# Norms over features through token columns: eight-column roots and reciprocals, spread back by TensorE

## Chip, cores and metric

The kernel runs on one core of a Trainium2 chip. The metric is the device time of one execution in microseconds (us), the median of several runs.

## The reference

Two transformer blocks follow each other on 1024 tokens of 1024 features, with 256 context tokens beside them. The norms and the residual sums around them are, cut down:

```python
def rms_norm(x, g):
    y = x * rsqrt(mean(x * x, axis=-1) + 1e-6)
    return y * g

# first block, its end
x = x + g1 * (y @ w_out)
x = x + g2 * swiglu(modulate(rms_norm(x, norm_ffn_g), sh2, sc2), w_ffn_in, w_ffn_out)
x = rms_norm(x, final_g)
# second block
h  = modulate(rms_norm(x, norm1), shift1, scale1)
hc = modulate(rms_norm(ctx, norm1), cshift, cscale)
# attention, state-space and grid branches of h and hc, then
x = x + gate1 * merged_branches
h2 = modulate(rms_norm(x, norm2), shift2, scale2)
x = x + gate2 * conv_ffn(h2, ...)
out = rms_norm(x, final_norm)
```

Each norm takes a mean over the features of one token, and there is a root and a reciprocal for each token.

## The kernel before

Features lie on the 128 partitions in eight blocks `k`, tokens along the free dimension, so x is 128 x 8192 and is worked on in pieces of 512 tokens (`LAT` is the two halves `n0` = 0 and 512; `ALL` adds the 256 context tokens in front). A sum over features is thus a sum over partitions and blocks. Each engine runs a program written by hand, stage after stage (`sp`, `act`, `dve`, `pool`, `pe` at the end of the file); the engines meet only at semaphores, `wait_ge(*stage.engine.after(key))`. An engine takes its instructions strictly in that order.

`SumSq` is the norm's sum. ScalarE squares block k of x into one of three buffers (`sqr`, a ring: a buffer is taken again when its last reader is through); GpSimd adds it to the square of block k-1 and so frees that one; when the eighth is added, TensorE multiplies the sum with a matrix of ones, so that the sum over partitions stands in every partition of a bank, 128 x 512; VectorE makes mean plus epsilon in `rsx`, ScalarE the root, VectorE the reciprocal, all on 512 columns.

The stages around it are: `op1` (output product, adds to x), `ffn1` (first feed-forward), `fn` (final norm of the first block, norm of the context and of the second block), `sx` (first products of the second block), and at the end `op2`, `ffn2` and the last norm (`last_dve`). In both products the float weights are cut into two parts, high by ScalarE (`wfh<-wslot`), low by VectorE (`wfl<-wslot,wfh`), into a ring of two, and each product is three matmuls. `Ffn` walks over tiles: `("u", f, 0)` and `("u", f, 1)` upward, then eight `("d", f, m)` downward for each group of four f; the last group has only two, so that its tiles are short: 12 matmuls. In these last eight tiles x is final block by block, and `SumSq` runs beside them. On ScalarE a tile m first cuts the weights of tile m+1, then squares block m of x:

```python
if i + 1 < len(self.tiles):
    self.cut_act(e, self.tiles[i + 1])
for n0, n in LAT:
    if kind == "d":
        if f + FP >= NF:
            self.ss.act(e, m, n0, n)
```

At a feed-forward's start `norm_dve` makes, for each half, the reciprocal, then for each k a product `t` (from `rsx`), which ScalarE shifts and rounds to `h`, and the rest `l`; TensorE's first tile waits for `l` of each k.

In `fn` VectorE first norms x in place with final_g (`x<-x,par,rsx`); the normed x is written to memory (`xspill`, read again by `op2`); the context is loaded, squared, summed; the normed x is squared and summed again; then the products `h<-x,gs,rsx` and ScalarE's shifts `h<-h,mod`. The first products of `sx` (`dtT`: 32 rows for context, half 0, half 1) follow on TensorE.

## Time and profile before

| | us |
|---|---|
| runs | 5033.08, 5028.90, 5030.50 |
| median | 5030.5 |
| profiled execution | 5029.09 |
| its span (core 0) | 5026.8 |
| TensorE busy in it | 4401.3 (88%) |
| VectorE busy | 2383.7 (47%) |
| ScalarE busy | 1396.0 (28%) |
| GpSimd busy | 983.2 (20%) |
| granted TensorE clock, mean | 0.935 of full |

The profiled execution is one run with the hardware profiler on; its span runs from the first to the last instruction, and the time adds what lies around it. Busy shares are over the whole span, so what an edit is worth must be read where it stands.

### The profile page before, as it was taken

Reading aid. Unit: us, or ns where it says so; the run is one execution under the profiler, and the core shown is the slowest. Engines: PE = TensorE matmul, PEld = TensorE weight load, DVE = VectorE, ACT = ScalarE, POOL = GpSimd, SP = SyncE. Lnnn points to the kernel's source line nnn. Section 1 sums busy time; section 2 is a strip of 40 time slices with the busy share of each in tenths; the row PEclk is TensorE's granted clock in tenths of the full one; section 3 lists DMA queues with packets and bytes.
Section 4 is the critical chain, followed back from the end, with each engine's and each line's share of the span. In section 5 each row is a group of like instructions: output and inputs, shape, how many; then the busy total and the mean of one; then the engine's idle time right before and its main releaser. Section 6 shows DMA issues by size and latency. Waiting matters only on the chain. (4 is left out here: it accounts for less than half of the span.)

```text
span 5026.8 us, 45510 instructions
## 1 busy us (share of the span) xinstructions
PE 4401.3 (88%) x18317; PEld 3044.0 (61%) x18317; DVE 2383.7 (47%) x3755; ACT 1396.0 (28%) x2601; POOL 983.2 (20%) x769
## 2 busy tenths in 40 slices
PE   7984788988899999587979998888797988999997
PEld 3454773675688888345554455555464656888885
DVE  2767745334555553335261105472675634333334
ACT  3431222112211111233231104352453533222222
POOL 0003443330244431305160100001000011000001
PEclk9996899999999999787979999999898999999998
DMA  5010032212233332102021110102000022111111
GB/s 180 25 59 17 28 103 90 59 59 73 66 109 113 114 105 61 58 27 75 17 76 34 34 43 18 37 22 80 13 20 23 20 70 71 51 49 44 51 42 59
DMA packets 245746, 288.34 MB, mean 57 GB/s; under 512 B 18112, under 2 KB 208896, under 8 KB 244256
## 3 DMA queue, kind: packets, MB, share of 16 engines
q1 hardware_dynamic: 227536, 203.51, 13.2%
q0 software_dynamic: 14880, 76.68, 4.8%
q10 hardware_dynamic: 3120, 5.24, 0.3%
...
## 5 line engine op out<-in xcount | busy, mean ns | idle before, releaser
L193 PE MATMUL bank<-h,wslot 128*128 128x512 f32 (+3 forms) x2096 | 906.1, 573 | 58.0 <-DMA wslot<-in_w_in 29.3
L193 PEld LDWEIGHTS bank<-h,wslot 128*128 128x128 f32 (+1 forms) x2096 | 382.2, 192 | 382.6 <-issue 364.9
L193 PE MATMUL bank<-hT,wslot 128*128 128x512 f32 (+3 forms) x1136 | 462.6, 564 | 38.0 <-DMA hT<-hspill 20.4
L193 PEld LDWEIGHTS bank<-hT,wslot 128*128 128x128 f32 (+1 forms) x1136 | 212.6, 190 | 266.3 <-issue 237.6
L193 PE MATMUL bank<-ffn1h,wfh 128*128 128x512 f32 x704 | 280.4, 398 | 18.8 <-DVE ffn1l L211 17.8
L193 PE MATMUL bank<-ffn2h,wgh 128*128 128x512 f32 x704 | 276.8, 393 | 17.3 <-DVE ffn2l L211 16.7
L211 DVE SCALAR_TENSOR_TENSOR x<-bank,mod,x 128x512 f32<-128x512 f32 x224 | 163.4, 745 | 246.8 <-PE bank L193 246.6
L193 PE MATMUL bank<-ffn1l,wfh 128*128 128x512 f32 x704 | 275.8, 392 | 0.0
L193 PE MATMUL bank<-ffn1h,wfl 128*128 128x512 f32 x704 | 275.2, 391 | 0.0
L193 PE MATMUL bank<-ffn2l,wgh 128*128 128x512 f32 x704 | 275.1, 391 | 0.0
L193 PE MATMUL bank<-ffn2h,wgl 128*128 128x512 f32 x704 | 275.1, 391 | 0.0
L205 DVE TENSOR_TENSOR wfl<-wslot,wfh 128x1024 fp32r<-128x1024 f32 (+2 forms) x92 | 155.4, 1689 | 159.8 <-ACT wfh L202 159.8
L205 POOL TENSOR_TENSOR sq<-sq 128x512 f32<-128x512 f32 (+1 forms) x91 | 112.2, 1233 | 427.2 <-ACT sq L202 423.2
L205 POOL TENSOR_TENSOR ffn2al<-ffn2ga,ffn2ah 128x512 fp32r<-128x512 f32 x44 | 57.4, 1305 | 662.0 <-ACT ffn2ah L202 662.0
L193 PEld LDWEIGHTS bank<-ffn1h,wfh 128*128 128x128 f32 x704 | 132.8, 189 | 52.3 <-DVE ffn1l L211 12.9
L226 DVE TENSOR_REDUCE at2a<-ffn1t 128x128 f32<-128x1024 f32 x72 | 143.2, 1988 | 44.2 <-POOL ffn1t L205 44.2
L193 PEld LDWEIGHTS bank<-ffn2h,wgh 128*128 128x128 f32 x704 | 132.7, 189 | 51.4 <-DVE ffn2l L211 13.0
L211 DVE SCALAR_TENSOR_TENSOR ffn2ga<-ffn2gw,par,ffn2ga 128x1024 f32<-128x1024 f32 x44 | 56.5, 1285 | 199.5 <-ACT ffn2ga L202 198.7
L193 PEld LDWEIGHTS bank<-ffn1h,wfl 128*128 128x128 f32 x704 | 133.0, 189 | 28.2
L193 PEld LDWEIGHTS bank<-ffn2h,wgl 128*128 128x128 f32 x704 | 132.9, 189 | 27.9
L193 PE MATMUL bank<-ffn1ah,wfh 128*128 128x512 f32 x352 | 142.8, 406 | 7.8 <-DVE wfl L205 7.1
L193 PEld LDWEIGHTS bank<-ffn2l,wgh 128*128 128x128 f32 x704 | 133.0, 189 | 26.7
...
## 6 DMA issues: line engine op xcount, KB each, us to landing
...
```

The lines of the kernel that those rows point to most:

```text
L193: return Counted() if counting[0] else self.q.matmul(o, l, r, start=start, stop=stop)
L205: return Counted() if counting[0] else self.q.tensor_tensor(o, a, b, op)
L211: return Counted() if counting[0] else self.q.scalar_tensor_tensor(o, a, s, b, op0, op1)
L226: return Counted() if counting[0] else self.q.reduce_sum(o, a, AX.X)
```

## The change

The sums change their form. TensorE now takes the squares as weights, 128 tokens at a time, and multiplies them with one column of ones: the result is a column of 128 token sums, one token per partition, and the 1024 tokens are eight columns of one bank. Mean, root and reciprocal work on 128 x 8. `spread_row` brings a column back to a row in every partition: the column, repeated 128 times, is the weight, the unit matrix the moving operand; four such matmuls fill 512 columns of a bank. The products then read this bank in place of `rsx`.

In `ffn1` (`SumSq2`) GpSimd's additions are left out: TensorE adds the blocks' columns up in one open bank during the last tiles, with two moving columns, ones and final_g squared, so that both the sum for the first norm and that for the norm after it come from the same squares. `fn` makes both reciprocals from them and applies both norms in one product; x stays as it was, is spilled in four parts during the last tiles, and `op2` norms it after loading it again. In both feed-forwards the squares of block m-1 are taken in tile m. In the products of `sx` the context comes last, and TensorE waits for each piece by itself. The context is loaded into buffers of `ffn1`, ahead of where the load stood.

```diff
+    def spread_row(e, rc, n0, n, b):
+        for c in range(n // 128):
+            i = e.matmul(b[:, hs[c]], rc[:, n0 // 128 + c:n0 // 128 + c + 1].to_broadcast([128, 128]), ident)
+        return i
...
+        def pe(self, e):
             for n0, n in LAT:
-                e.wait_ge(*self.st.pe.after("sum", n0))
-                e.tensor_scalar(rsx[:, n0:n0 + n], self.bk[n0 // 512][:, 0:n], 1.0 / D, EPS, OP.mult, OP.add).then_inc(self.st.dve("ms", n0), 1)
+                e.wait_ge(*self.st.pool.after("sq", n0, 7))
+                for c in range(4):
+                    i = e.matmul(bank[6][:, n0 // 128 + c:n0 // 128 + c + 1], sqr[self, n0, 7][:, hs[c]], ones[:, 0:1])
+                i.then_inc(self.st.pe("sum", n0), 1)
+                sqr.give((self, n0, 7), self.st.pe.now())
+            e.wait_ge(*self.st.dve.after("rs"))
+            for n0, n in LAT:
+                spread_row(e, self.rc, n0, n, self.row(n0)).then_inc(self.st.pe("row", n0), 1)
+        def dve(self, e):
+            e.wait_ge(*self.st.pe.after("sum", 512))
+            e.tensor_scalar(self.rc[:, :], bank[6][:, 0:8], 1.0 / D, EPS, OP.mult, OP.add).then_inc(self.st.dve("ms"), 1)
+            e.wait_ge(*self.st.act.after("rt"))
+            e.reciprocal(self.rc[:, :], self.rc[:, :]).then_inc(self.st.dve("rs"), 1)
...
+            e.wait_ge(*self.st.dve.after("ms"))
+            e.activation(self.rc[:, :], self.rc[:, :], AF.Sqrt).then_inc(self.st.act("rt"), 1)
+        def row(self, n0):
+            return bank[7 - n0 // 512]
 
         def rs(self, n0):
-            return self.inv.after("rs", n0)
+            return self.st.pe.after("row", n0)
...
+    class SumSq2(SumSq):
+        def pe_tile(self, e, k, n0, n):
+            if k == 0 and n0 == 0:
+                e.wait_ge(*fn.dve.after("g2"))
+                e.matmul(bank[6][:, 0:16], ident, C("offF", 112, 128), start=True, stop=False).then_inc(self.st.pe("zero"), 1)
+            e.wait_ge(*self.st.act.after("sq", n0, k))
+            for c in range(4):
+                at = (n0 // 128 + c) * 2
+                i = e.matmul(bank[6][:, at:at + 2], sqr[self, n0, k][:, hs[c]], gf2[:, k * 2:k * 2 + 2], start=False, stop=k == 7 and at == 14)
+            i.then_inc(self.st.pe("sum", n0, k), 1)
+            sqr.give((self, n0, k), self.st.pe.now())
...
+                prep(e, j)
...
-                self.ss_in.dve_inv(e, n0, n)
                 e.wait_ge(*d.after("gs"))
                 e.wait_ge(*self.ss_in.rs(n0))
                 for k in range(8):
                     tmp = self.tr.take(k, n0)
                     for ev in self.tr.freed(k, n0):
                         e.wait_ge(*ev)
-                    e.stt(tmp[:, 0:n], self.x(k, n0, n), gs1[:, k:k + 1], rsx[:, n0:n0 + n], OP.mult, OP.mult).then_inc(d("t", k, n0), 1)
+                    e.stt(tmp[:, 0:n], self.x(k, n0, n), gs1[:, k:k + 1], self.ss_in.row(n0)[:, 0:n], OP.mult, OP.mult).then_inc(d("t", k, n0), 1)
...
+                if kind == "d" and f + FP >= NF and m >= 2 and not self.conv:
+                    for n0, n in LAT:
+                        self.ss.pe_tile(e, m - 2, n0, n)
+            if self.conv:
+                self.ss.pe(e)
+            for m in () if self.conv else (6, 7):
+                for n0, n in LAT:
+                    self.ss.pe_tile(e, m, n0, n)
...
-                        if f + FP >= NF:
-                            self.ss.act(e, m, n0, n)
+                        if f + FP >= NF and m:
+                            self.ss.act(e, m - 1, n0, n)
...
-            self.ss.act_root(e)
+            for n0, n in LAT:
+                self.ss.act(e, 7, n0, n)
+            if self.conv:
+                self.ss.act_root(e)
...
+                    elif m % 2:
+                        e.wait_ge(*st.dve.after("x", f, m, 512))
+                        e.dma_start(io["xspill"][:, (m - 1) * NL:(m + 1) * NL], x1[:, (m - 1) * NL:(m + 1) * NL]).then_inc(xs_out(m), 16)
...
     def fn_sp(e):
+        barrier(e, at2.st)
+        for i in range(2):
+            e.dma_start(cx[i][:, :].rearrange("p (k t) -> p k t", t=CT), io["ctx2T"][:, i * 4:i * 4 + 4, :]).then_inc(cx_in(i), 16)
...
+        S = bank[6][:, 0:16].rearrange("p (c w) -> p c w", w=2)
+        e.tensor_scalar(rn1[:, :], S[:, :, 0], 1.0 / D, EPS, OP.mult, OP.add).then_inc(d("v1"), 1)
+        e.stt(gsc[:, :], ad2.mv[:, 8:16, 1], 1.0, P("norm1_2"), OP.add, OP.mult).then_inc(d("gsc"), 1)
+        e.stt(ggs[:, :], ad2.mv[:, 8:16, 0], 1.0, P("norm1_2"), OP.add, OP.mult).then_inc(d("gs"), 1)
+        e.wait_ge(*a.after("s1"))
+        e.reciprocal(rn1[:, :], rn1[:, :]).then_inc(d("r1"), 1)
+        e.wait_ge(*d.now())
+        e.tensor_tensor(rn2[:, :], S[:, :, 1], rn1[:, :], OP.mult).then_inc(d("q1"), 1)
+        e.wait_ge(*d.now())
+        e.tensor_tensor(rn2[:, :], rn2[:, :], rn1[:, :], OP.mult).then_inc(d("q2"), 1)
+        e.wait_ge(*d.now())
+        e.tensor_scalar(rn2[:, :], rn2[:, :], 1.0 / D, EPS, OP.mult, OP.add).then_inc(d("v2"), 1)
+        e.tensor_tensor(ggs[:, :], ggs[:, :], P("final_g"), OP.mult).then_inc(d("ggs"), 1)
+        e.wait_ge(*a.after("s2"))
+        e.reciprocal(rn2[:, :], rn2[:, :]).then_inc(d("r2"), 1)
+        e.wait_ge(*d.now())
+        e.tensor_tensor(rn12[:, :], rn2[:, :], rn1[:, :], OP.mult).then_inc(d("r12"), 1)
...
+        def ctx():
+            e.wait_ge(*fn.pe.after("cs"))
+            e.tensor_scalar(rcc, bank[4][:, 0:2], 1.0 / D, EPS, OP.mult, OP.add).then_inc(d("vc"), 1)
+            e.wait_ge(*a.after("sc"))
+            e.reciprocal(rcc, rcc).then_inc(d("rc"), 1)
         for n0, n in LAT:
-            e.wait_ge(*fn.dve.after("x", 7, n0))
-        e.dma_start(io["xspill"], x1[:, :]).then_inc(xs_out("out"), 16)
-        rms_c.pool(e)
-        for n0, n in LAT:
+            e.wait_ge(*fn.pe.after("row", n0))
             for k in range(8):
-                ss_f.pool(e, k, n0, n)
-    def fn_dve(e):
-        barrier(e, ffn1.st, ffn1.ss.st, at2.st)
-        for n0, n in LAT:
-            ffn1.ss.dve_inv(e, n0, n)
-            e.wait_ge(*ffn1.ss.rs(n0))
+                e.stt(hv2(k, CT + n0, n), X1(k, n0, n), ggs[:, k:k + 1], bank[7 - n0 // 512][:, 0:n], OP.mult, OP.mult).then_inc(d("h", CT + n0, k), 1)
+            if n0 == 0:
+                ctx()
+        e.wait_ge(*fn.pe.after("rowc"))
+        for k in range(8):
+            e.stt(hv2(k, 0, CT), XC(k), gsc[:, k:k + 1], bank[5][:, 0:CT], OP.mult, OP.mult).then_inc(d("h", 0, k), 1)
...
+    def fn_act(e):
+        d, a = fn.dve, fn.act
+        barrier(e, ffn1.st, at2.st)
+        e.wait_ge(*d.after("v1"))
+        e.activation(rn1[:, :], rn1[:, :], AF.Sqrt).then_inc(a("s1"), 1)
+        e.wait_ge(*cx_in.after(1))
+        def squares(ks):
+            for k in ks:
+                sq = sqr.take("cx", k)
+                for ev in sqr.freed("cx", k):
+                    e.wait_ge(*ev)
+                e.activation(sq[:, 0:CT], XC(k), AF.Square).then_inc(a("cq", k), 1)
+        squares(range(2))
+        e.wait_ge(*d.after("v2"))
+        e.activation(rn2[:, :], rn2[:, :], AF.Sqrt).then_inc(a("s2"), 1)
+        squares(range(2, 8))
+        e.wait_ge(*d.after("vc"))
+        e.activation(rcc, rcc, AF.Sqrt).then_inc(a("sc"), 1)
+        for n0, n in ALL[1:] + ALL[:1]:
             for k in range(8):
-                a = X1(k, n0, n)
-                e.stt(a, a, P("final_g", k, k + 1), rsx[:, n0:n0 + n], OP.mult, OP.mult).then_inc(fn.dve("x", k, n0), 1)
-        rms_c.dve(e)
-        e.wait_ge(*fn.dve.now())
-        ss_f.dve_mean(e)
-        for n0, n in LAT:
-            ss_f.dve_inv(e, n0, n)
-        nm_l.dve(e)
-        nm_c.dve(e)
-    def fn_act(e):
-        barrier(e, ffn1.st, ffn1.ss.st, at2.st)
-        e.wait_ge(*cx_in.after("in"))
-        rms_c.squares(e)
-        rms_c.roots(e)
-        for n0, n in LAT:
-            for k in range(8):
-                ss_f.act(e, k, n0, n)
-        ss_f.act_root(e)
-        nm_l.act(e)
-        nm_c.act(e)
+                e.wait_ge(*d.after("h", n0, k))
+                h = hv2(k, n0, n)
+                e.activation(h, h, AF.Identity, bias=ad2.mv[:, k, 0 if n0 else 1:1 if n0 else 2]).then_inc(a("h", n0, k), 1)
...
+        e.matmul(bank[4][:, 0:2], ident, C("offF", 112, 114), start=True, stop=False).then_inc(fn.pe("zero"), 1)
+        for k in range(8):
+            if k == 2:
+                e.wait_ge(*fn.dve.after("r12"))
+                for n0, n in LAT:
+                    spread_row(e, rn12, n0, n, bank[7 - n0 // 512]).then_inc(fn.pe("row", n0), 1)
+            e.wait_ge(*fn.act.after("cq", k))
+            for c in range(2):
+                i = e.matmul(bank[4][:, c:c + 1], sqr["cx", k][:, hs[c]], ones[:, 0:1], start=False, stop=k == 7 and c == 1)
+            i.then_inc(fn.pe(*(("cs", k) if k < 7 else ("cs",))), 1)
+            sqr.give(("cx", k), fn.pe.now())
+        e.wait_ge(*fn.dve.after("rc"))
+        spread_row(e, rcc, 0, CT, bank[5]).then_inc(fn.pe("rowc"), 1)
...
-                for n0, n in ALL:
+                for n0, n in ALL[1:] + ALL[:1]:
                     b = bk.take("dtT", n0)
+                    e.wait_ge(*h2_ready(n0))
...
+        def norm(e, j):
+            for n0, n in LAT:
+                a = X2r(j, n0, n)
+                e.wait_ge(*ln.pe.after("row", n0))
+                e.stt(a, a, P("final_g", j, j + 1), bank[7 - n0 // 512][:, 0:n], OP.mult, OP.mult).then_inc(ln.dve("x1", j, n0), 1)
+            e.wait_ge(*ln.dve.now())
+        op2.dve(e, lambda: x2_in.after("in"), norm)
...
+            spread_row(e, rn1, n0, n, bank[7 - n0 // 512]).then_inc(ln.pe("row", n0), 1)
...
-            ffn2.ss.dve_inv(e, n0, n)
             e.wait_ge(*ffn2.ss.rs(n0))
             for k in range(8):
                 a = X2r(k, n0, n)
-                e.stt(a, a, P("final_norm_2", k, k + 1), rsx[:, n0:n0 + n], OP.mult, OP.mult).then_inc(ln.dve("x", k, n0), 1)
+                e.stt(a, a, P("final_norm_2", k, k + 1), ffn2.ss.row(n0)[:, 0:n], OP.mult, OP.mult).then_inc(ln.dve("x", k, n0), 1)
```

How this moves instructions is seen in the order of each engine. TensorE, the end of `ffn1` (tile 2 and the beginning of tile 3; `wfh` and `wfl` are the cut weights), of the changed kernel:

```order
L193 MATMUL bank<-ffn1ah,wfh 128x512
L193 MATMUL bank<-ffn1al,wfh 128x512
L193 MATMUL bank<-ffn1ah,wfl 128x512
L193 MATMUL bank<-cst 128x16
L193 MATMUL bank<-gf,sq 128x2 x8
L193 MATMUL bank<-ffn1ah,wfh 128x512
L193 MATMUL bank<-ffn1al,wfh 128x512
L193 MATMUL bank<-ffn1ah,wfl 128x512
```

Between the matmuls of two tiles there now stand eight with two columns, for the squares of the block two tiles back; before, matmuls of 512 columns alone stood here.

ScalarE from the last cut of `ffn1` to the first shift (`rsx`, `rcx`, `rcs`, `gs` in this place are means of which the root is taken; `cx` is the context, which lies in `ffn1t` after the change), before:

```order
L202 ACTIVATE wfh<-wslot 128x256
L202 ACTIVATE sq<-x 128x512 x4
L202 ACT_TABLE_LOAD
L202 ACTIVATE rsx<-rsx 128x512 x2
L202 ACTIVATE sq<-cx 128x256 x8
L202 ACTIVATE rcx<-rcx 128x256
L202 ACTIVATE sq<-x 128x512 x16
L202 ACTIVATE rsx<-rsx 128x512 x2
L202 ACTIVATE h<-h,mod 128x512 x16
```

and of the changed kernel:

```order
L202 ACTIVATE wfh<-wslot 128x256
L202 ACTIVATE sq<-x 128x512 x6
L202 ACT_TABLE_LOAD
L202 ACTIVATE rcs<-rcs 128x8
L202 ACTIVATE sq<-ffn1t 128x256 x2
L202 ACTIVATE rcs<-rcs 128x8
L202 ACTIVATE sq<-ffn1t 128x256 x6
L202 ACTIVATE gs<-gs 128x2
L202 ACTIVATE h<-h,mod 128x512 x16
```

The sixteen second squares of x are gone, and the root for the context (`gs<-gs`) stands in front of the shifts. VectorE in front of `ffn1`, the piece of difference:

```order
-L208 TENSOR_SCALAR rsx<-bank 128x512 x2
+L208 TENSOR_SCALAR rcs<-bank 128x8
+L217 RECIPROCAL rcs<-rcs 128x8
+L214 COPY gf<-cst 128x8
+L205 TENSOR_TENSOR gf<-par 128x8
 L205 TENSOR_TENSOR wfl<-wslot,wfh 128x1024
 L211 SCALAR_TENSOR_TENSOR gs<-mod,par 128x8
-L217 RECIPROCAL rsx<-rsx 128x512
-L211 SCALAR_TENSOR_TENSOR ffn1t<-x,gs,rsx 128x512 x2
+L211 SCALAR_TENSOR_TENSOR ffn1t<-x,gs,bank 128x512 x2
```

The reciprocal moved from behind the weights' cut to ahead of it, and has 8 columns.

## Rows read from the trace of the kernel before

**Rows 1.** Windows view, all engines, over four stretches (us from the start).

```profile
core 0 of [0], span 5026.8 us
core 0: us, PE busy (x) PEld busy (x) DVE busy (x) ACT busy (x) POOL busy (x), PEclk, DMA share, GB/s
...
2047.40:2067.40 20.00, 15.30 (x49) 10.98 (x48) 10.45 (x12) 6.11 (x13) 10.21 (x8) 0.83 0.05 14
2074.00:2154.80 80.80, 8.71 (x11) 2.33 (x11) 43.61 (x53) 31.95 (x56) 25.95 (x25) 0.52 0.21 80
...
4998.70:5026.80 28.10, 3.70 (x4) 1.00 (x4) 19.43 (x21) 4.09 (x6) 3.78 (x3) 0.62 0.40 149
```

**Rows 2.** Timeline between the blocks, 2109 to 2155 us.

```profile
2109.74 9.70 POOL L205 TENSOR_TENSOR sq<-sq 128x512 f32<-128x512 f32 x7 [3.37 <-ACT sq L202]
...
2140.07 10.69 DVE L211 SCALAR_TENSOR_TENSOR h<-x,gs,rsx 128x512 f32<-128x512 f32 x16
2140.85 13.85 ACT L202 ACTIVATE h<-h,mod 128x512 f32<-128x512 f32 x24 [6.72 <-DVE h L211]
...
2154.80 29.87 PE L193 MATMUL bank<-h,wslot 128*32 128x256 f32 x80 [22.06 <-ACT h L202]
```

**Rows 3.** Timeline, one tile of ffn1's end, 2059 to 2064 us.

```profile
2059.29 0.50 PE L193 MATMUL bank<-ffn1ah,wfh 128*128 128x512 f32 x1 [2.00 <-DVE wfl L205]
...
2059.99 0.63 ACT L202 ACTIVATE sq<-x 128x512 f32<-128x512 f32 x1 [2.07 <-DVE x L211]
...
2060.70 1.28 POOL L205 TENSOR_TENSOR sq<-sq 128x512 f32<-128x512 f32 x1 [1.75 <-ACT sq L202]
...
2062.01 0.63 ACT L202 ACTIVATE sq<-x 128x512 f32<-128x512 f32 x1 [1.39 <-POOL sq L205]
...
2062.55 0.40 ACT L202 ACTIVATE wfh<-wslot 128x256 fp32r<-128x256 f32 x1
...
2062.98 1.31 DVE L205 TENSOR_TENSOR wfl<-wslot,wfh 128x256 fp32r<-128x256 f32 x1 [2.42 <-ACT wfh L202]
```

**Rows 4.** Timeline of TensorE at two places; the tile view of rt, its reciprocal.

```profile
371.00 1.06 PE L193 MATMUL bank<-cst,gg 128*128 128x128 f32 x8
...
1343.35 0.39 PE L193 MATMUL bank<-ffn1h,wfl 128*128 128x512 f32 x1
1343.58 0.28 PE L193 MATMUL bank<-cst,at2a 128*128 128x1 f32 x2
...
1344.03 0.40 PE L193 MATMUL bank<-ffn1l,wfh 128*128 128x512 f32 x1
...
L217 DVE RECIPROCAL rt<-rt x1: 203/203/203, 817.9 to 817.9; 128x8 f32<-128x8 f32 x1
```

**Rows 5.** Timeline in front of ffn1, 1295 to 1306 us.

```profile
1295.50 1.13 PE L193 MATMUL bank<-sq,cst 128*128 128x512 f32 x2 [2.04 <-POOL sq L205]
...
1297.39 0.63 ACT L202 ACTIVATE rsx<-rsx 128x512 f32<-128x512 f32 x1 [1.34 <-DVE rsx L208]
...
1300.87 1.23 DVE L205 TENSOR_TENSOR wfl<-wslot,wfh 128x1024 fp32r<-128x1024 f32 x1 [3.52 <-ACT wfh L202]
...
1302.09 3.34 DVE L217 RECIPROCAL rsx<-rsx 128x512 f32<-128x512 f32 x1
1305.54 1.41 DVE L211 SCALAR_TENSOR_TENSOR ffn1t<-x,gs,rsx 128x512 f32<-128x512 f32 x2
```

**Rows 6.** Timeline of the last 25 us.

```profile
5003.01 1.28 ACT L202 ACT_TABLE_LOAD   x1
5003.07 1.26 POOL L205 TENSOR_TENSOR sq<-sq 128x512 f32<-128x512 f32 x1 [0.74 <-ACT sq L202]
...
5018.80 5.39 DVE L211 SCALAR_TENSOR_TENSOR x<-x,par,rsx 128x512 f32<-128x512 f32 x8
```

**Rows 7.** VectorE's groups by line: products from the bank, and from SBUF.

```profile
L211 DVE SCALAR_TENSOR_TENSOR x<-bank,mod,x 128x512 f32<-128x512 f32 x224 | 163.4, 745 | 246.8 <-PE bank L193 246.6
...
L211 DVE SCALAR_TENSOR_TENSOR x<-x,par,rsx 128x512 f32<-128x512 f32 x32 | 21.6, 747 | 0.1
```

94 lines of the change are left out of this document (40 added, 54 removed).

## The prediction

> **What bounds the kernel now.** I read the windows view first. TensorE works for most of the span, so time can only leave where it stands still or runs slowly. Four such stretches touch the change [rows 1]: the last tiles of each feed-forward (49 matmuls in 20.0 us, about 12 to a tile, so 5.0 us a tile at granted clock 0.83), the 80.8 us between the blocks, in which TensorE is busy for 8.7 us, and the last 28.1 us. The same kind of gap, shorter, stands in front of each feed-forward [rows 5].
>
> The timeline then says what each gap waits for. Between the blocks the work is one line of dependences: a norm applied to x in place, a second set of squares, whose GpSimd sums of the first half alone take 9.70 us, reciprocals over 512 columns, then sixteen products (10.69 us) and ScalarE's shifts [rows 2]. TensorE restarts at 2154.80, after all 24 shifts. In the last feed-forward tiles a cycle runs over three engines [rows 3]: ScalarE squares (2059.99), GpSimd adds (to 2061.98), only then is a square buffer free for the next square (2062.01), behind which ScalarE cuts the next weights (2062.55), VectorE's cut ends at 2064.29, and TensorE, which finished the tile before, starts. A half costs 2.02 us of square and sum. In front of a feed-forward a reciprocal of 3.34 us stands between the weight cut and the first product, and another between the halves [rows 5].
>
> **A, op1 into ffn1.** The order rows show two 512-column reciprocals replaced by one of 8 columns. A reciprocal on 8 columns took 0.203 us [rows 4]. The sum becomes four matmuls per half. The one-column matmuls of the trace are the same thing: two records of 128x1 push the matmul after next to 0.68 us behind, where two spacings of 0.23 are 0.45, so a matmul costs 0.23 and four cost 0.9 [rows 4]; the old sum took 1.13. The mean takes about 0.2 instead of 0.7 us, the root about 0.25 instead of 0.63. The last root then ends near 1296.9 instead of 1298.02. Behind it on ScalarE stand a table load, two small activations and the cut; all move 1.1 us up. VectorE's cut still follows, but the first product follows it directly: the 3.45 us from 1302.09 to 1305.54 go [rows 5]. The second half starts with no reciprocal: 3.4 us more, in full, since VectorE's products pace TensorE in both halves. The spread of the reciprocal (eight matmuls, two records each, of the form that shows 8 records in 1.06 us [rows 4]: some 2 us) lies beside the cut; without that cover it would cost 1.0 for the first half. A = 1.1 + 3.45 + 3.4 = **7.9 us**.
>
> **C, op2 into ffn2.** The same pattern stands at 4240 to 4252 without the table load: **7.8 us**. The 16 added products that norm the reloaded x in op2 cost 16 x 0.67 = 10.8 us of VectorE (eight end within 5.39 us [rows 6]), at most 1.4 us a tile; a tile is 48 matmuls at 0.23, 11 us, of which VectorE fills under 4. I cost them at nothing; uncovered they would cost up to 10.8. The eight spread matmuls at op2's start stand before VectorE has cut the first weights.
>
> **B, the last tiles of ffn1 and the stage between the blocks.** GpSimd leaves the cycle, and squares are taken a tile later, behind the next cut. Now TensorE sets the pace: 12 matmuls at 0.23 are 2.75 us and eight square sums at 0.23 are 1.8 us, 4.55 a tile against 5.0. So removing the wait gains little here; the matmuls that replace GpSimd take it back. At 2047.4 three tiles are through; from there 5 x 2.75 + 8 x 1.8 = 28.15 us gives 2075.5, where the old last matmul ended at 2074.0. If the clock stays at 0.83, that is up to 5.8 us more, if it is full, none; the work is denser than before, so I take 2: 2077.5.
>
> Then nine small steps on 8 columns (mean, root, reciprocal, two products, mean, root, reciprocal, product) at 0.2 [rows 4] plus a hand-over each: 2.0 to 3.5, taken 2.5: 2080.0. The first row of four matmuls is 1.0 to 2.0 at the two clock levels, taken 1.6: 2081.6. Eight products at 10.69/16 = 0.67: 2087.0 [rows 2]. Here the order rows matter: ScalarE has the root for the context (`gs<-gs`) **ahead** of all shifts, and VectorE makes that root's input only after its eight products. So no shift starts until about 2087.5, and the eight shifts run after the products instead of beside them. Their own pace is between 13.85/24 = 0.58 and 0.67 [rows 2]; at 0.62, 5.0 us: TensorE starts the dt products at **2092.5**. It no longer waits for the second half or the context, since they now come in that order. The second half's products and shifts, 5.4 and 5.0 us, lie beside the first dt product. B = 2154.8 - 2092.5 = **62.3 us**; the bounds, taken together, give 2088.8 and 2098.2, so 66.0 and 56.6. The spill of x, four DMAs issued by GpSimd in the last tiles, and the context load, moved ahead of the next block's weights on SP's queue, are not waited for by anything before 2078; I cost them at nothing. Uncovered, the squares of the context would begin late, which is what the chain's root for the context waits for.
>
> **D, the end.** In ffn2 GpSimd keeps the sums, and its half of 2.02 us is now the pace: 4.0 us a tile for 5.0, over the five tiles that were paced by the cycle: 5.0 us. From the last sum (5003.07 + 1.26 = 5004.33) to the end were 22.5 us [rows 6]. Now: sums 1.6, mean 0.2, root 0.3, reciprocal 0.4, first row 1.6, hand-overs 0.3, sixteen products at 0.67 in a row 10.8, and the 2.6 us from the last product to the end: 17.8. The table load stays in the shadow of the sum, as now: it runs at 5003.01, before its root has an input [rows 6]. D = 5.0 + 4.7 = **9.7 us** (8.3 to 11, with sums and row at either clock).
>
> A product that reads its row from the matmul's bank is costed like one from SBUF: 745 ns against 747 [rows 7]. The Trainium skill says otherwise: "VectorE: DVE Perf Modes", "The TRN2 errata — SBUF-src ops pay a fixed extra latency per instruction", gives a fixed 120 cycles from PSUM and 58 from SBUF, an estimate of 0.065 us more each by that page. By it 56 products on the path would add 3.6 us; the trace does not show this on an operation that reads one of each.
>
> **The sum.** 7.9 + 62.3 + 7.8 + 9.7 = 87.7 us off the profiled execution, whose time is 5029.1 (span 5026.8): 4941.4. The median of the runs lies 1.4 above that time, so **4943 us**.
>
> **Rivals.**
> - The square sums cost twice the 0.23 each, because their weights change at every matmul and, unlike the single one-column matmul of the trace, there are eight in a row with no long matmul to cover the loads: a tile becomes 2.75 + 3.7 = 6.4 us, slower than the 5.0 of before, and ffn1's end comes 8 x 1.8 = 14 us later. Against it, the back-to-back form with 8 records in 1.06 us [rows 4]. 4957 us. Chance 0.10.
> - Reading the bank costs VectorE 0.065 us more where both operands matter: 56 x 0.065 = 3.6: 4946. Chance 0.10.
> - Full clock in ffn1's end and short hand-overs: 4 us off in B, 2 in A and C, 1.5 in D, and up to 4 more: 4930 to 4936. Chance 0.08.
> - The next stage is not ready so early: its first weights are issued behind ffn1's last cuts, and 70 us of cover go. If they or the spill's 4 MB come late: some 7 us, 4950. Chance 0.05.
> - Slower than before: TensorE starts the next stage at the lower level and stays there. A matmul of 512 columns would take twice 0.23; the 87.7 us are gone after 380 of them, 175 us at 1.2 GHz on end. The trace shows low clock only in the gaps and just behind them [rows 1]. Over 5031 us. Chance 0.02.
> - No change, since another wait ends the gap: nothing else in the stretch reaches 2154 without the second set of squares. Chance 0.01.
>
> **How the numbers follow.** The forecast, with its own bounds (A and C 7 to 8.5 each, B 56.6 to 66.0, D 8.3 to 11), spans 4937 to 4951 and has 0.64. The range for 8 in 10 must reach the square-sum rival in part and the faster case: **4932 to 4957**. Faster by over 0.2% (10 us, about what a measurement of this kernel tells from no change): 0.97; within: 0.01; slower: 0.02.
>
> **What would show it.** In the trace of the changed kernel: `bank<-gf,sq` groups of 16 records lasting about 1.8 us; a tile of 4.55 us at ffn1's end and 4.0 at ffn2's; ScalarE idle until the root on `gs`, then 16 shifts without a gap; the first 32x512 dt product near 2084.6 on the new clock of the trace, since all of it lies 7.9 us earlier by then; the first product 3.4 us behind the cut's end no longer. I am wrong in B if a tile at ffn1's end takes over 5 us, or if shifts run beside the products; in D if the last 16 products are interrupted by their rows or the output DMA ends later than 2.6 us behind them.

## The result, and the profile after

The changed kernel takes **4962.5 us** (median of 4 runs, 4956.4 to 4966.4) where the kernel before takes 5030.6 (4 runs, 5028.9 to 5033.1): a ratio of 0.986, 95% interval 0.985 to 0.988. Faster, as predicted, but 68 us and not 88: the median lies 19.5 us above the predicted 4943 and outside the range. The profiled execution is the fastest of the four, 4956.4 us with a span of 4954.6; against its own forecast of 4941.4 it is 15.0 too long.

The windows view of the changed kernel, for the stretches of [rows 1]: ffn1's last tiles, 20.3 us up to the first dt product of the second block, and the end from ffn2's last x product. The columns are those of [rows 1].

```profile
2047.70:2067.70 20.00, 20.00 (x124) 17.74 (x125) 7.71 (x12) 7.36 (x14) 1.08 (x2) 1.00 0.69 241
2075.00:2095.26 20.26, 14.24 (x65) 13.74 (x66) 12.00 (x28) 9.96 (x21) 0.00 (x0) 0.50 0.00 0
4927.60:4954.60 27.00, 7.51 (x32) 7.05 (x32) 11.74 (x19) 4.01 (x6) 5.72 (x5) 0.66 0.42 155
```

TensorE is busy all the time at ffn1's end and at clock 1.0. The 80.8 us from ffn1's last x product to the first dt product have become 25.5 (2069.76 to 2095.26), from 2073 on at clock 0.50. The timeline in front of ffn1, which answers to [rows 5]:

```profile
1299.98 0.21 ACT L202 ACTIVATE rcs<-rcs 128x8 f32<-128x8 f32 x1 [2.20 <-DVE rcs L208]
1300.22 0.20 DVE L217 RECIPROCAL rcs<-rcs 128x8 f32<-128x8 f32 x1 [0.28 <-ACT rcs L202]
1300.48 3.79 PE L193 MATMUL bank<-cst,rcs 128*128 128x128 f32 x16 [0.74 <-DVE rcs L217]
1304.36 0.17 DVE L214 COPY gf<-cst 128x8 f32<-128x8 f32 x1 [3.93 <-PE bank L193]
1304.41 1.28 ACT L202 ACT_TABLE_LOAD   x1 [4.22 <-PE bank L193]
...
1306.99 1.22 DVE L205 TENSOR_TENSOR wfl<-wslot,wfh 128x1024 fp32r<-128x1024 f32 x1 [2.39 <-ACT wfh L202]
...
1308.33 1.41 DVE L211 SCALAR_TENSOR_TENSOR ffn1t<-x,gs,bank 128x512 f32<-128x512 f32 x2
```

The reciprocal is done at 1300.42, and then VectorE and ScalarE both stand for 4 us, although nothing that they do next (a copy, a table load, the weight cut) reads a row. They wait at `barrier(e, op1.st, op1.sp2.st)`: the row events are now counted in the stage of the sum, so the barrier asks for all eight spread products. Those take 3.8 us. The same stands in front of ffn2:

```profile
4185.41 0.20 DVE L217 RECIPROCAL rcs<-rcs 128x8 f32<-128x8 f32 x1 [0.27 <-ACT rcs L202]
...
4189.37 1.06 ACT L202 ACTIVATE wgh<-wslot 128x1024 fp32r<-128x1024 f32 x1 [3.99 <-PE bank L193]
...
4190.56 1.23 DVE L205 TENSOR_TENSOR wgl<-wslot,wgh 128x1024 fp32r<-128x1024 f32 x1 [4.95 <-ACT wgh L202]
...
4191.89 1.40 DVE L211 SCALAR_TENSOR_TENSOR ffn2t<-x,gs,bank 128x512 f32<-128x512 f32 x2
```

Between the blocks, which answers to [rows 2]:

```profile
2069.55 7.50 PE L193 MATMUL bank<-gf,sq 128*128 128x2 f32 x48
...
2077.25 0.17 DVE L208 TENSOR_SCALAR rcs<-bank 128x8 f32<-128x8 f32 x1 [6.74 <-PE bank L193]
2077.51 1.28 ACT L202 ACT_TABLE_LOAD   x1 [4.56 <-DVE gsc L211]
2078.81 0.21 ACT L202 ACTIVATE rcs<-rcs 128x8 f32<-128x8 f32 x1
...
2080.38 0.17 DVE L205 TENSOR_TENSOR rcs<-rcs 128x8 f32<-128x8 f32 x1
2081.10 3.76 PE L193 MATMUL bank<-cst,rcs 128*128 128x128 f32 x16
...
2083.20 5.36 DVE L211 SCALAR_TENSOR_TENSOR h<-x,ggs,bank 128x512 f32<-128x512 f32 x8 [2.65 <-PE bank L193]
...
2085.54 0.42 ACT L202 ACTIVATE sq<-ffn1t 128x256 f32<-128x256 f32 x1 [3.85 <-PE bank L193]
...
2089.81 0.16 DVE L208 TENSOR_SCALAR gs<-bank 128x2 f32<-128x2 f32 x1 [1.26 <-PE bank L193]
2090.01 0.20 ACT L202 ACTIVATE gs<-gs 128x2 f32<-128x2 f32 x1 [2.34 <-DVE gs L208]
2090.11 13.08 ACT L202 ACTIVATE h<-h,mod 128x512 f32<-128x512 f32 x24
...
2095.26 30.15 PE L193 MATMUL bank<-h,wslot 128*32 128x512 f32 x80 [3.57 <-ACT h L202]
```

The table load stands behind the wait for the mean, on the chain. The last of the nine small steps ends at 2080.55, but the rows start only at 2081.10, behind the sums of two context squares. While the two rows go over TensorE, the context's squares wait for a buffer that only TensorE's sums free (3.85 us), so VectorE waits 1.26 us for the context's sum, and every shift waits for its root.

The end, which answers to [rows 6]:

```profile
4935.01 1.26 POOL L205 TENSOR_TENSOR sq<-sq 128x512 f32<-128x512 f32 x1 [0.74 <-ACT sq L202]
...
4938.23 0.17 DVE L208 TENSOR_SCALAR rcs<-bank 128x8 f32<-128x8 f32 x1 [9.87 <-PE bank L193]
...
4941.04 10.62 DVE L211 SCALAR_TENSOR_TENSOR x<-x,par,bank 128x512 f32<-128x512 f32 x16 [2.17 <-PE bank L193]
```

**Where the 72.2 us between the two profiled spans lie**, by events that both traces have:

| stretch | before | after | gained | predicted |
|---|---|---|---|---|
| start to op1's last x product | 1292.63 | 1295.01 | -2.4 | 0 |
| to the second weight cut of ffn1 | 38.65 | 35.61 | 3.0 | A 7.9 |
| to ffn1's last x product | 742.76 | 739.14 | 3.6 | B 62.3 with the next |
| to the first addition to dt | 111.97 | 56.98 | 55.0 | |
| to op2's last x product | 2054.19 | 2054.27 | -0.1 | 0 |
| to the second weight cut of ffn2 | 37.23 | 33.18 | 4.1 | C 7.8 |
| to ffn2's last x product | 721.26 | 713.43 | 7.8 | D 9.7 with the next |
| to the end of the span | 28.11 | 26.98 | 1.1 | |

A lacks 4.9 us, B 3.7, C 3.7, D 0.7, and 2.4 were lost ahead of op1's last x product, in stages that are the same in both kernels.

### The profile page after: what moved, and what is told of

Same layout as the page of the kernel before. It is cut to its first block and busy times, and to the rows that moved or that the text cites. A ratio compares the mean times of both kernels' runs of the same rounds, so it can differ in the third digit from the quotient of the medians.

```text
span 4954.6 us, 45959 instructions
## 1 busy us (share of the span) xinstructions
PE 4425.1 (89%) x18591; PEld 3083.2 (62%) x18591; DVE 2340.3 (47%) x3751; ACT 1379.5 (28%) x2580; POOL 946.5 (19%) x737
## 5 line engine op out<-in xcount | busy, mean ns | idle before, releaser
L193 PE MATMUL bank<-ffn1h,wfh 128*128 128x512 f32 x704 | 279.9, 398 | 11.7 <-DVE ffn1l L211 10.9
L193 PEld LDWEIGHTS bank<-ffn1h,wfh 128*128 128x128 f32 x704 | 132.7, 188 | 44.6 <-DVE ffn1l L211 10.5
L193 PEld LDWEIGHTS bank<-ffn1l,wfh 128*128 128x128 f32 x704 | 132.8, 189 | 25.3
L205 POOL TENSOR_TENSOR sq<-sq 128x512 f32<-128x512 f32 x56 | 71.7, 1280 | 396.4 <-ACT sq L202 394.8
## 6 DMA issues: line engine op xcount, KB each, us to landing
hT<-hspill POOLq DMA_DIRECT2D x2, 5120.0 KB, 15.6
```

The lines of the kernel that those rows point to most:

```text
L193: return Counted() if counting[0] else self.q.matmul(o, l, r, start=start, stop=stop)
L205: return Counted() if counting[0] else self.q.tensor_tensor(o, a, b, op)
```

## The experiments

Each is one edit of the changed kernel. The whole time of an execution scatters by some 10 us, so besides the time (median, with the ratio to the kernel before on the same chip) the table gives stretches of each profiled trace, which repeat far better (F moves by up to 2 us with the clock): **A** from op1's last x product to ffn1's first norm product, **F** from ffn1's last x product to the first addition to dt, **C** from op2's last x product to ffn2's first norm product, **T** from there to ffn2's last x product, **D** from that to the first output product.

| kernel | A | F | C | T | D | time | ratio |
|---|---|---|---|---|---|---|---|
| changed | 13.3 | 57.0 | 10.9 | 735.7 | 13.4 | 4962.5 | 0.986 [0.985, 0.988] |
| changed, again | 13.1 | 57.0 | 10.9 | 735.8 | 13.4 | 4955.6 | 0.985 [0.983, 0.986] |
| e1 rows apart | 9.5 | 57.0 | 7.4 | 735.8 | 13.4 | 4946.9 | 0.983 [0.981, 0.984] |
| e2 root behind | 13.1 | 54.0 | 10.8 | 735.8 | 13.4 | 4953.3 | 0.984 [0.983, 0.986] |
| e3 table early | 13.2 | 54.1 | 11.0 | 735.8 | 13.4 | 4953.3 | 0.984 [0.983, 0.986] |
| e4 last square | 13.1 | 57.0 | 10.6 | 735.8 | 15.6 | 4963.6 | 0.985 [0.984, 0.987] |
| e5 fill | 10.8 | 55.9 | 9.4 | 735.8 | 17.1 | 4953.4 | 0.984 [0.982, 0.985] |
| e6 same tile | 13.3 | 57.0 | 11.1 | 743.6 | 10.5 | 4963.5 | 0.986 [0.984, 0.987] |
| e7 = e1 + cut in the shadow | 7.7 | 55.4 | 6.9 | 735.9 | 13.4 | 4946.1 | 0.982 [0.981, 0.984] |
| e9 five squares | 13.2 | 57.0 | 10.8 | 732.2 | 8.3 | 4948.8 | 0.984 [0.983, 0.986] |
| e10 fill placed | 10.8 | 55.4 | 9.4 | 735.8 | 13.4 | 4948.6 | 0.984 [0.982, 0.985] |
| e11 row later | 13.3 | 54.6 | 11.0 | 735.8 | 13.4 | 4957.0 | 0.985 [0.983, 0.987] |
| e12 = e2 + e3 | 13.3 | 53.5 | 11.1 | 735.8 | 13.4 | 4954.3 | 0.985 [0.983, 0.986] |
| b1 all | 7.7 | 52.2 | 6.8 | 732.3 | 7.8 | 4935.2 | 0.981 [0.980, 0.982] |
| b2 all + fill | 5.9 | 53.9 | 5.9 | 732.3 | 9.5 | 4938.0 | 0.982 [0.980, 0.983] |
| b3 all + fill at op1, op2 | 5.9 | 54.7 | 5.9 | 732.3 | 7.8 | 4934.7 | 0.980 [0.979, 0.982] |

**The changed kernel again.**

> The changed kernel once more, unchanged. If the 10 us between its runs so far (4956.4 to 4966.4) are the kernel's own scatter, the new median lies within 4 us of 4962.5, and the profiled execution need not be 2.4 us behind the kernel before where op1 ends: that offset arose in stages which are the same in both, and is chance. If it comes from the change (tiles at other addresses, say), the x products of op1 end 2 to 3 us later than in the kernel before again.

Median 4955.6 (4 runs, 4952.4 to 4961.0), 7 us below the first and so outside the 4 that I had allowed. The ratios, 0.986 [0.985, 0.988] and 0.985 [0.983, 0.986], overlap. op1's last x product ended up at 1289.88, 5.1 us earlier than in the first trace of the same kernel and 2.8 earlier than in the kernel before: the 2.4 us of the table's first line are chance. The stretch from dt to op2's last x product, too, takes 2052.0 to 2061.4 us over these traces. Two traces that differ nowhere in their code there, e1 and e7, show in the windows view of TensorE one such place:

```profile
3410.00:3425.00 15.00, 12.61 (x92) 1.00 0.38 107
```
```profile
3410.00:3425.00 15.00, 12.60 (x65) 0.89 0.36 107
```

The granted clock is 1.00 in the first and 0.89 in the second, and across that place e7 falls 1.6 us back.

**The barrier (e1).**

```diff
+            self.rw = Sem(nm + "_row")
-   spread_row(e, self.rc, n0, n, self.row(n0)).then_inc(self.st.pe("row", n0), 1)
+   spread_row(e, self.rc, n0, n, self.row(n0)).then_inc(self.rw(n0), 1)
-            return self.st.pe.after("row", n0)
+            return self.rw.after(n0)
```

> The two row events of SumSq count on a semaphore of their own, which the barriers at the start of ffn1 and ffn2 don't ask for; who reads the rows still waits for them. Theory (the barrier makes both cuts of the first weight tile wait for all eight spread products): from op1's last x product to ffn1's first norm product 13.3 us becomes 8.9 to 9.5, in front of ffn2 10.9 becomes 7.9 to 8.5, the end of the program (no stage behind it) stays at 18.3; in all 6.5 to 7.5 us less than the changed kernel. Rival (the eight spread products and the small sums at the low clock are the price themselves, whoever waits): the cut moves ahead, but the first norm product still waits for its row, and the two places give back 0 to 1.5 us together.

A 9.5, C 7.4 (I had expected 7.9 to 8.5), F and D unchanged: 7.1 us together against the repeated run, and 8.8 in the medians. The timeline of e1 in front of ffn1:

```profile
1297.49 3.78 PE L193 MATMUL bank<-cst,rcs 128*128 128x128 f32 x16 [0.74 <-DVE rcs L217]
1297.61 1.28 ACT L202 ACT_TABLE_LOAD   x1 [0.41 <-DVE rcs L217]
...
1299.12 1.04 ACT L202 ACTIVATE wfh<-wslot 128x1024 fp32r<-128x1024 f32 x1
1300.19 1.23 DVE L205 TENSOR_TENSOR wfl<-wslot,wfh 128x1024 fp32r<-128x1024 f32 x1 [2.42 <-ACT wfh L202]
...
1301.53 1.41 DVE L211 SCALAR_TENSOR_TENSOR ffn1t<-x,gs,bank 128x512 f32<-128x512 f32 x2
```

The spread still takes 3.8 us, but beside table load and cut. The rival, that the spread itself is the price whoever waits, falls: it left 0 to 1.5 us for the two places together.

**Two orders in fn (e2, e3).**

```diff
-        e.wait_ge(*d.after("vc"))
-        e.activation(rcc, rcc, AF.Sqrt).then_inc(a("sc"), 1)
         for n0, n in ALL[1:] + ALL[:1]:
             ...
+            if n0 == CT:
+                e.wait_ge(*d.after("vc"))
+                e.activation(rcc, rcc, AF.Sqrt).then_inc(a("sc"), 1)
```

> In fn the root of the context's norm stands on ScalarE behind the first eight shifts and no longer ahead of them. Theory (ScalarE's order holds the shifts up, and with them the first dt product): the shifts follow their products from about 6 us after the first, the last of eight ends 0.6 us behind the eighth product, VectorE waits 1 us or less for the root, and the first dt product starts 3 to 4 us earlier (2095.3 becomes about 2091.5), with the time 3 to 4 us less. Rival (VectorE's wait for the root and the row of the context on TensorE, which stands ahead of the first dt product, take it back): 0 to 1 us.

F falls by 3.0, at the lower end of what I expected; from the mean to the first dt product 18.0 us become 15.4, and I had put 3 to 4 there. The timeline of e2: the shifts begin 2.9 us behind the first product (they still wait for the context's squares ahead of them on ScalarE), VectorE's wait for the root is longer than I expected, 2.60 us, and the first dt product no longer waits for a shift: it starts right behind the context's row, which stands ahead of it on TensorE although it doesn't read it. So a part of the rival holds; no run moves that row.

```profile
2077.76 5.36 DVE L211 SCALAR_TENSOR_TENSOR h<-x,ggs,bank 128x512 f32<-128x512 f32 x8 [2.66 <-PE bank L193]
2080.67 4.99 ACT L202 ACTIVATE h<-h,mod 128x512 f32<-128x512 f32 x8
2085.78 0.17 DVE L217 RECIPROCAL gs<-gs 128x2 f32<-128x2 f32 x1 [2.60 <-ACT gs L202]
...
2086.01 1.22 PE L193 MATMUL bank<-cst,gs 128*128 128x128 f32 x4 [4.36 <-DVE gs L217]
2087.16 5.26 PE L193 MATMUL bank<-h,wslot 128*32 128x512 f32 x6
```

```diff
+    tb = sb("tb", [1])
         barrier(e, ffn1.st, at2.st)
+        e.activation(tb[:, :], ones[:, 0:1], AF.Sqrt).then_inc(a("tb"), 1)
         e.wait_ge(*d.after("v1"))
```

> In fn a square root of one column of ones, read by nobody, stands ahead of ScalarE's wait for the mean, so that the table of the root is loaded while ffn1's last sums run. Theory (the load of 1.28 us stood behind the wait, on the chain): mean to root 1.56 becomes 0.3, and all of fn behind it starts 1.3 us earlier. Rival (the load is repeated by the squares of the context between the roots, or the wait was covered by TensorE's sums): less than 0.3 us.

From the mean to the last of the nine steps it takes 1.76 us instead of 3.13, as expected. The first of the eight products starts 1.1 us earlier behind the mean (4.83 us for 5.95): the sums of two context squares still stand ahead of the rows. But to the first dt product the gain is 2.5 (18.0 to 15.5), not 1.3: VectorE's wait of 1.26 us for the context's sum is gone too. The windows view shows why: TensorE's clock while it sums the context's squares, first in the changed kernel, then in e2.

```profile
2084.00:2087.00 3.00, 3.00 (x17) 0.50 0.00 0
```
```profile
2079.00:2082.00 3.00, 2.65 (x25) 1.00 0.00 0
```

In e3 it is 0.96 as well. Up to these sums e2's instructions are the changed kernel's, so there the clock's return is not the edit's doing, and part of both gains may not be either. ScalarE loads the table at 2070.09 in e3, the mean comes at 2074.05. The Trainium skill, "ScalarE: Activation LUTs", "What ACT_TABLE_LOAD costs", gives 1283 ns for the load and 1380 ns of drain with it; the trace agrees on the load (1.28) and shows no drain: moving it made those nine steps 1.37 us shorter.

**What is order and what is clock in fn (e11, e12).** e11 spreads the second half's row behind the context's sums; e12 is e2 and e3 together.

```diff
-                for n0, n in LAT:
-                    spread_row(e, rn12, n0, n, bank[7 - n0 // 512]).then_inc(fn.pe("row", n0), 1)
+                spread_row(e, rn12, 0, 512, bank[7]).then_inc(fn.pe("row", 0), 1)
...
             sqr.give(("cx", k), fn.pe.now())
+        spread_row(e, rn12, 512, 512, bank[6]).then_inc(fn.pe("row", 512), 1)
```

> In fn TensorE spreads only the first half's row where both stood; the second half's row follows behind the context's sums. Theory (VectorE's 1.26 us wait for the context's sum, which holds up the root and all shifts, comes from the second row standing ahead of those sums): the wait goes, and from the mean to the first dt product 18.0 us becomes 16.7 to 16.9, with TensorE's clock as low as in the changed kernel. Rival (the sums are slow by the clock and by ScalarE's squares, whatever stands ahead of them, or the later second row costs as much): 17.7 to 18.0.

Mean to first dt product 16.65 us, with the sums at the low clock:

```profile
2082.80 5.12 PE L193 MATMUL bank<-cst,sq 128*128 128x1 f32 x24
...
2088.32 0.15 DVE L208 TENSOR_SCALAR gs<-bank 128x2 f32<-128x2 f32 x1
```

The wait for the context's sum is gone by order alone: 1.36 us.

> The early table and the root behind the first eight shifts together. In each alone TensorE's clock was back at 1.0 when it summed the context's squares (2.74 us for 5.12 in the changed kernel), so that part of their 3 us may be the clock's. Theory (the two orders are worth 1.4 and 1.1 us by themselves, the clock 1.3 more where it happens to be back): from the mean to the first dt product 18.0 becomes 15.4 to 15.7 if the context's sums take 5.1 us, and 13.9 to 14.3 if they take 2.7. Rival (the orders alone make the whole of it): 12.5 to 13, at either clock.

14.35 us with sums of 2.74, just above the 13.9 to 14.3 that the theory said for that clock. The rival (12.5 to 13) falls. How the 3.65 us divide into order and clock, these runs don't measure: neither the changed kernel nor e12 has a trace at the other clock. The one pair with the same instructions in fn at both clocks is b1 and b3 (below), 15.0 and 16.7 us; by its 1.6 I estimate some 2.0 for the two orders together.

**The last square straight to TensorE (e4).** GpSimd adds only up to block 6; behind its sum the last square goes into the same eight columns:

```diff
-            if k:
+            if 0 < k < 7:
...
+            e.wait_ge(*self.st.act.after("sq", 0, 7))
+            e.matmul(bank[6][:, 0:8], ident, C("offF", 112, 120), start=True, stop=False).then_inc(self.st.pe("zero"), 1)
...
+                for k in (6, 7):
+                    e.wait_ge(*(self.st.pool if k == 6 else self.st.act).after("sq", n0, k))
```

> GpSimd no longer adds the last square of each half in op1, op2 and ffn2; TensorE sums the six-tile sum and the last square one behind the other into the same eight columns. Theory (the GpSimd addition of 1.26 us and its hand-over stand on the chain between the last x product and the mean): last x product to mean 1.3 us shorter at three places (4.8 to 3.5 in front of ffn1, 4.0 to 2.7 in front of ffn2, and 13.4 to 12.1 from ffn2's last x product to the first output product), 3.5 to 4 us in all. Rival (twice as many small products on TensorE, in part at the low clock, of 0.23 us each, take its place): 0 to 1 us.

A miss. A and C gain 0 to 0.3, and D grows by 2.2, a loss that the rival did not forecast either. The timeline of e4's end:

```profile
4939.11 6.97 PE L193 MATMUL bank<-cst,sq 128*128 128x1 f32 x32
4946.12 0.17 DVE L208 TENSOR_SCALAR rcs<-bank 128x8 f32<-128x8 f32 x1 [12.08 <-PE bank L193]
```

Sixteen small matmuls at the low clock take 7.0 us, 0.44 each, more than the additions that they replace; the rival had priced them at 0.23. The edit has a second fault: TensorE waits for the first half's last square (5.42 us idle, to 4938.67) before it opens the bank, although GpSimd had that half's sum of seven blocks ready at 4935.95. So this run shows that the edit as written loses, not that its idea must.

**Fill products (e5, e10).** Wide products into a bank that nobody reads, in TensorE's waits (the cut shows those behind op1, op2 and ffn2; three and four more stand in fn):

```diff
+    def fill(e, b, n):
+        for i in range(n):
+            e.matmul(b[:, :], ident, cst[:, 0:512])
...
                 sqr.give((self, n0, 7), self.st.pe.now())
+                fill(e, bank[7], 2 if n0 == 0 else 1)
```

> Products of 128x512 into a bank that nobody reads fill TensorE's waits behind op1, op2 and ffn2 (two, then one) and in fn (three ahead of the context's sums, four behind the context's row). Theory (TensorE's clock of 1.2 GHz in these stretches is what makes the eight spread products 3.8 us, ffn1's and ffn2's small sums 1.9 us and the first dt product 9 us): with the waits filled the granted clock stays at 1.0 there, the eight spread products take about 2 us and the first dt product under 7.5, and the time falls by 5 to 8 us. Rival (a fill product under way makes what comes behind it late, and the clock falls all the same): the stretches keep their lengths or grow by 1 to 3 us each.

Both theories have their places. The timeline of e5 in front of ffn1 and in fn, and the windows view of 1300 to 1302:

```profile
1299.91 1.99 PE L193 MATMUL bank<-cst,rcs 128*128 128x128 f32 x16
...
2073.12 5.89 PE L193 MATMUL bank<-cst 128*128 128x2 f32 x8 [0.36 <-PE bank L193]
2081.16 5.35 DVE L211 SCALAR_TENSOR_TENSOR h<-x,ggs,bank 128x512 f32<-128x512 f32 x8 [4.92 <-PE bank L193]
```
```profile
1300.00:1302.00 2.00, 1.90 (x17) 1.70 (x16) 0.01 (x1) 0.00 (x0) 0.00 (x0) 1.00 0.00 0
```

In front of ffn1 the clock stays at 1.00 and the eight spread products take 1.99 us instead of 3.79; A gains 2.4 and C 1.5. In fn and at the end the fills ran at the low clock, some 1.8 to 2.0 us each, and stood in the way: the rows came later, from the mean to the first dt product 18.0 us became 21.2, and D grew by 3.7. F is shorter all the same (55.9), because the mean came 5.4 us behind the last x product for 7.5, ahead of all fills in fn.

> Fill products again, without those in fn, and in ffn2's end six ahead of the wait for GpSimd's last additions, where TensorE is idle for 6.8 us, and one between the halves. Theory (the low clock doubles small sums and spread products, and a fill costs only where it is still under way when the awaited value comes): in front of ffn1 2.4 and in front of ffn2 1.5 us less than in the changed kernel, as in the first fill run; from ffn2's last x product to the first output product 13.4 becomes 11.5 to 12; fn as in the changed kernel; in all 5 to 6 us less. Rival for the end (the clock falls there whatever TensorE does, or fills make the sums late): the end gains nothing.

A and C as in e5. At the end six fills ran ahead of the sums and one behind each half. The sums did get faster (the second 1.14 us), but the last fill itself took 2.05 us when the clock fell under it, and the row waited:

```profile
4924.44 1.14 PE L193 MATMUL bank<-cst,sq 128*128 128x1 f32 x8
4925.45 2.05 PE L193 MATMUL bank<-cst 128*128 128x512 f32 x2
4927.29 2.62 PE L193 MATMUL bank<-cst,rcs 128*128 128x128 f32 x16
```

D stays at 13.4, as the rival for the end said. Both of its reasons have a part, with one difference: the clock fell under the last fill, and it was the row, not the sums, that the fill made late.

**ffn2's squares in their own tile (e6)**, as in the kernel before: `if f + FP >= NF and (m or self.conv): self.ss.act(e, m if self.conv else m - 1, n0, n)`.

> In ffn2 alone ScalarE squares a tile in the tile's own turn again, as the kernel before does, and not a tile later. Theory (with the square in its own turn ScalarE's cut of the tile after next waits for the x products, and the last round's tiles take 5.0 us for 4.0): ffn2's last x product comes 5 us later and the time is 5 us above the changed kernel's. Rival (it was the shorter sums behind the end, or the cadence of GpSimd at 2.02 us a half, that gave the gain): 0 to 1 us.

T grows by 7.8 us and D shrinks by 3.0, since fewer squares are left behind the last x product: 4.9 together, the 5.0 that the prediction gave this edit. Its timeline shows the cycle of [rows 3] again, ScalarE waiting for x, then for GpSimd, then cutting:

```profile
4910.86 0.63 ACT L202 ACTIVATE sq<-x 128x512 f32<-128x512 f32 x1 [2.07 <-DVE x L211]
4912.90 0.63 ACT L202 ACTIVATE sq<-x 128x512 f32<-128x512 f32 x1 [1.40 <-POOL sq L205]
4913.44 0.40 ACT L202 ACTIVATE wgh<-wslot 128x256 fp32r<-128x256 f32 x1
```

**The cut in the shadow (e7)**, on top of e1; the same for ffn2, and root and mean leave op1's and op2's programs:

```diff
     def ffn1_dve(e):
-        barrier(e, op1.st, op1.sp2.st)
+        barrier(e, op1.st)
         fn_g2(e)
         ffn1.cut_dve(e, ffn1.tiles[0])
+        op1.sp2.dve(e)
+        barrier(e, op1.sp2.st)
```

> On top of the rows' own semaphore, ScalarE and VectorE cut the next stage's first weight tile ahead of the root and the mean, while GpSimd and TensorE still finish the sums; ad2's two activations stand behind the root. Theory (with the barrier mended the cut of 1.04 and 1.23 us is what the first norm product waits for, not its row): op1's last x product to ffn1's first norm product 9.5 becomes 7.5 to 8, op2's to ffn2's 7.4 becomes 6.2 to 6.6 (by then the row is what ends it), 2.5 to 3.5 us less than with the semaphore alone. Rival (the cut makes root and mean late, or the load of the activation table that the other function needs takes the place): under 1 us.

A 7.7, C 6.9: 2.4 us less than e1 (C a little less than expected). What ends the wait now is the row:

```profile
1302.92 1.41 DVE L211 SCALAR_TENSOR_TENSOR ffn1t<-x,gs,bank 128x512 f32<-128x512 f32 x2 [2.03 <-PE bank L193]
```

**Five square buffers in ffn2 (e9).** The two new ones are the halves of `rsx`.

```diff
+   self.sqr = Ring(sqr.bufs + [rsx[:, 0:512], rsx[:, 512:1024]]) if nm == 'ffn2_ss' else sqr
```

> ffn2's sums take five buffers for their squares in place of three (the two new ones are the halves of a tile that nobody uses in that stage). Theory (in ffn2's last round ScalarE's square waits for the addition just before it to free its buffer, and that loop of square 0.63, addition 1.26 to 1.29 and hand-overs is the 2.02 us a half that bound it): GpSimd's additions follow each other at 1.3 to 1.5 us, the last one ends 7 to 9 us earlier and so does the first output product. Rival (the additions slow down beside VectorE, or the tiles are bound by TensorE and the cuts): 1 to 3 us.

T 3.5 less, D 5.1 less, 8.6 in all. The changed kernel's GpSimd rows stand 2.00 us apart with 0.74 idle before each; e9's follow each other at 1.25 to 1.45:

```profile
4911.37 0.42 ACT L202 ACTIVATE wgh<-wslot 128x256 fp32r<-128x256 f32 x1 [1.26 <-PE bank L193]
4917.83 2.55 POOL L205 TENSOR_TENSOR rsx<-rsx,sq 128x512 f32<-128x512 f32 x2 [0.17 <-ACT rsx L202]
```

ScalarE's cut now waits for TensorE, which paces the tiles at 2.72 us for the changed kernel's 4.05.

**All together (b1), and with fills (b2).** b1 also sends fn's two rows ahead of all of the context's sums (`if k == 0` for `if k == 2`).

> Together: the rows' own semaphore, the cuts ahead of root and mean, five buffers in ffn2, and in fn the early table, the context's root behind the first eight shifts and the two rows ahead of all of the context's sums. By the stretches measured so far: op1's last x product to the first norm product 7.7, op2's 6.9, fn 5 to 6 us shorter than in the changed kernel (1.3 table, 3 to 4 shifts, 1 rows no longer behind sums), the end 7 to 9 shorter if the buffers do it: 21 to 24 us less, near 4937. Rival (fn's gains overlap, since the first dt product then waits for TensorE's sums of the context): 17 to 19.

> The same with the fill products at op1's and op2's ends, and one ahead of ffn2's sums. Theory (with the cuts in the shadow the row is what the first norm product waits for, and a row costs half at the full clock): another 1 to 2 us at each of the two places, 0.5 to 1 at the end, 3 to 4 us below the one without. Rival (the last fill is still under way when root or sum is ready): within 1 us of it.

b1: 5.7 off A, 4.8 off F, 4.0 off C, 3.4 off T, 5.6 off D, 23.5 us by the stretches against the changed kernel's first trace. Not all of it is the edits': 2.0 of F's 4.8 lie between the last x product and the mean, where b1 changes nothing, and behind the mean the context's sums ran at clock 0.9. Its median of 4935.2 (4 runs, 4928.6 to 4939.7) is 20 below the changed kernel's repeated run. b2 gains 2.6 more at A and C and loses 1.7 of it at the end, where e10 gained nothing, and as much in F, ahead of the mean. Its median is not the expected 3 to 4 us below b1's but 2.8 above, and its stretches add up to 0.7 more: the rival's outcome.

> All together, with fill products at the ends of op1 and op2 alone. Theory (there a fill ends before the awaited value and keeps the clock; at ffn2's end it does not): A 5.9 and C 5.9 as in the version with all fills, the end at 7.8 as in the one without; 2 to 3 us below that one by the stretches, if fn's stretch stays between 52 and 54. Rival (the clock kept at op1's end is lost somewhere behind it): the sum of the stretches is within 1 us of the version without.

A and C are 5.9 and the end 7.8, but F is 54.7 for b1's 52.2, with the same instructions in that stretch: from ffn1's last x product to the mean 7.0 us for 5.5, and the context's sums at half clock, so that the first dt product stands 16.7 us behind the mean for 15.0. The five stretches add up to 806.5 for b1's 806.8: the rival's outcome. I can't say that the fills at op1 caused the earlier fall of the clock 770 us later; over all traces last x product to mean takes between 5.4 and 7.6 us without regard to the edit. The medians of b1 and b3 (4935.2 and 4934.7) don't tell the two apart, and both beat the two kernels; b1 does it with fewer instructions.

## Why the prediction was off

**A and C: "the spread lies beside the cut" was wrong.** I read the order of the instructions, in which no row stands ahead of the cut, and not what the cut waits for. The barrier in front of the stage asks for the last event of the sum's stage, and the change had put the rows into it. I had also priced the eight spread products at 2 us, by a row at full clock [rows 4]; at 1.2 GHz they were 3.8. In front of ffn1 the first half gained nothing: from op1's last x product to the first norm product 13.3 us for 12.9 before. The reciprocal's 3.34 us were paid back as the wait; only the second half's 3.4 arrived. e1 removes the wait and gives back 3.6 and 3.5 us; counted against the kernel before, A is then 6.9 and C 7.5, for 7.9 and 7.8.

The 1.0 us that A still lacks is its first term, the root that was to end 1.1 us earlier. It ended 5.18 us behind the last x product for 5.39 before, since the second half's sum ran at clock 0.50 and took 1.87 us for the 0.9 of my sum. In front of ffn2 the same sum took 1.05 us, and there the root did end 1.0 earlier.

**B: the mechanism was right, three small terms were short.** On the clock of the kernel before (the changed trace is 0.7 us ahead at ffn1's second cut): ffn1's square sums cost what I said (its last x products stand 4.57 us apart from tile to tile; I had 4.55) and the mean stands at 2077.9 for 2077.5. The 2 us that I had added for the clock were used up by the last 24 sums, 7.50 us for 5.5; that they matched is luck, since over all traces this stretch moves by 2.2 us. The nine steps took 3.3 us for 2.5, because the table load of 1.28 us stood on the chain; for the end of the kernel I had looked where it stands, for fn not. From there to the first product 2.65 us passed for 1.6, all at clock 0.50: 0.55 behind the sums of two context squares, 2.1 for the row. VectorE waited 1.26 us for the context's sum, which I had put at nothing: I had named the order that makes ScalarE's root hold up the shifts, but not that the rows hold up the sums in front of it. The eight shifts took 5.0 as predicted. Together the first dt product stood at 2095.9 for 2092.5. e3 takes 1.37 us out of the first of these terms, of which 1.1 reach the products; e11 takes out the third (1.36). The second is mostly the clock, and no run of the changed kernel alone changes that.

**D was right**: 9.0 for 9.7. The last sum to the end of the span took 18.3 us for 17.8: the small sums 2.0 instead of 1.6 and the first row 2.2 instead of 1.6, both at the low clock, against 0.3 less in mean, root and reciprocal. The pace of 2.02 us a half was named rightly too; e9 shows that it was the ring of three buffers that set it.

**The 16 added products in op2 cost nothing**: a tile of op2 takes 10.88 us in both kernels. (The stretch from the dt addition to op2's last x product, 2054.27 us for 2054.19, scatters by 9 us and shows it less well.) **The bank** costs VectorE nothing either: eight products that read their row from the bank end within 5.36 us, for 5.39 where it lies in SBUF [rows 6]. The Trainium skill, "VectorE: DVE Perf Modes", "The TRN2 errata — SBUF-src ops pay a fixed extra latency per instruction", would have it slower by 62 cycles; by that page's figures the eight would take an estimated 0.5 us more, and the trace disagrees, for products that read one operand from each.

**From the profiled execution to the median** the prediction added 1.4 us; here it was 6.1. Over both sets the changed kernel's eight runs lie between 4952.4 and 4966.4. The range was worked out from the terms of one execution and held nothing for this. The repeated set's median, 4955.6, would have lain inside the range: whether a set falls in or out is chance here, but that 13 us of the predicted gain are missing is not, for the stretches show them.
